# Token-row pairs of 512 columns for the gates, the branch products, the output and the HGRN values of a hybrid decoder layer

## The chip, the core and the metric

The kernel runs on one NeuronCore of a Trainium2 chip. The metric is the device time of one execution in microseconds (us). Lower is better.

## What is computed

One layer reads `x` (256 tokens, 1024 channels), normalises it, multiplies it by one wide input projection, runs three token mixers on slices of the result, gates them, projects each of them, merges the three with sigmoid gates, projects again, normalises and adds `x`. Cut to what matters here:

```
h = rms_norm(x, pre_norm)
z = einsum('btd,dn->btn', h, w_in)                 # 12,848 columns
o_a = nsa_mixer(...)  * silu(a_silu)               # sparse attention, 16 heads
o_b = pool_mixer(...) * silu(b_silu)               # causal pooling
o_c = rms_norm(hgrn2_mixer(q, f_logits, inp, lb))  * silu(c_silu)   # gated recurrence, values inp
y = einsum('btnc,ncd->btnd', stack([o_a, o_b, o_c]), w_branch)
gates = sigmoid(merge_logits)                      # 3 x 1024 columns of z
merged = sum(gates * y)
out = einsum('btd,de->bte', merged, w_out)
x = x + rms_norm(out, post_norm)
```

Everything is float32. A product that has to keep float32 precision is made of three passes on split operands: a value is rounded to a high part (`hH`, `bH`, `WH`) and the rest is a low part (`hL`, `bL`, `WL`), and the product is H times WL plus L times WH plus H times WH.

## The kernel before

The weights are read in 67 slabs, numbered s = 0 to 66 in the order of the list that `plan_slabs` writes. A slab is 1 MB: 1024 rows by 256 columns (`SLAB`), and its product with the 256 tokens is 48 matmuls (2 halves c, 8 row blocks k of 128, 3 passes j). Two slabs at s = 16 and 17, `vwk` and `vw`, are cut the other way: each has half of the rows (4 blocks) of the same 304 columns, so the two together are one product, and each is 24 matmuls.

A product can be laid out in two ways. Feature-major: the weight block is the stationary operand, the 256 tokens stream through, and the result has channels on partitions. Token-major (the kinds in `TOKEN_MAJOR`): 128 tokens of `hH` or `hL` are stationary, the weight columns stream through, and the result has token rows on partitions.

The work of a slab is spread over the engines, each with its own queue, in the order of s:

- SyncE (SP) loads slab s + 3 into `W` when the slab that used the place has been split.
- ScalarE (ACT) makes the high part `WH` (`hi`, L452), and in `read` takes the finished product out of PSUM: a copy, a tanh for the gates (L601) or a square for the last norm (L608). Per slab it runs `mix(s)`, then `read(s)`, then `hi(s + 3)`.
- VectorE (DVE) makes the low part `WL` (`lo`, L662) and the rest of the reads: the SiLU product (L865, L875), the gated branch product (L885) and, in the last branch, its addition to the merged sum `M` (L890).
- GpSimd (POOL) adds the gated products of the first two branches into `M` (`add_merged`, L427), and scales attention probabilities (L414, L417).
- TensorE (PE) runs `mix(s)`, the small matmuls of the mixers, and then `product(s)` (L1030). The recurrence has its turns from s = 9 to 24, the attention heads from s = 32 to 50.

Slab s writes PSUM bank s % 2, so a product waits until slab s - 2 has been read. `M` is held with channels on partitions. Before the output projection, which needs channels on partitions as its stationary operand, `merged_hi` (L546) and `merged_lo` (L756) split `M` into `hH` and `hL`. From s = 51 on no mixer is left: 4 SiLU slabs, then merge and branch slabs in turn up to s = 62, then 4 output slabs. Behind the last product stand, for each of the two token halves, a square (L644), a sum (L964), the product with the norm's gain (L965), a root (L646), a reciprocal (L967), two scaled additions (L970) and the stores.

Of the kernel before, what the change touches and what calls it, by code (L numbers as in the profile page):

```python
# [36 lines left out]
HALF_K = KC // 2  # L37

# [32 lines left out]
LAST = NS - 5  # L71
# [5 lines left out]
ACT_READS = [sum(x[0] in BY_ACT for x in SLABS[:i + 1]) for i in range(NS)]  # L77
DVE_READS = [sum(x[0] in BY_DVE for x in SLABS[:i + 1]) for i in range(NS)]
# [15 lines left out]
def trunk(nc, x, small, consts, w_in, cmp_w, pool_w, w_branch, w_out, post_norm, out):  # L94
# [14 lines left out]
    with ctx:  # L109
# [60 lines left out]
        M = R[:, 3, :].rearrange("p (c t) -> p c t", c=KC)  # L170
# [66 lines left out]
        s_px, s_gg = sem("pool_out"), sem("gates_done")  # L237
        s_fin, s_lbd, s_fin_ss = sem("final"), sem("lb_ready"), sem("out_squares")
# [3 lines left out]
        def slab_source(s):  # L242
# [4 lines left out]
            if kind in TWO_BANKS:  # L247
                part = D // 2 * TWO_BANKS.index(kind)
                return src[part:part + D // 2, col:col + WIDE].rearrange("(k p) n -> p k n", p=P)
            return src[:, col:col + SLAB].rearrange("(k p) n -> p k n", p=P)  # L250

        def slab_view(slot, s):

            if SLABS[s][0] in TWO_BANKS:
                return slot.rearrange("p k n -> p (k n)")[:, 0:HALF_K * WIDE].rearrange("p (k n) -> p k n", n=WIDE)
# [11 lines left out]
        def last_rows(i):  # L267

            return ps[:, (NS - 1) % 2 if i == 0 else 2, 0:SLAB]
# [70 lines left out]
        def _(pool):  # L340
# [80 lines left out]
            def add_merged(b, n):  # L421
                k = 4 * (2 - b) + n
                pool.wait_ge(s_read_v, DVE_READS[WHERE[("branch", n, b)]])
                m = M[:, 2 * n:2 * n + 2, :].rearrange("p c t -> p (c t)")
                if b < 2:
                    pool.wait_ge(s_madd, k - 3)
                    pool.tensor_tensor(m, m, U, ALU.add).then_inc(s_madd, 1)  # L427
                else:
                    pool.tensor_copy(m, U).then_inc(s_madd, 1)
# [10 lines left out]
        def _(act):  # L440
# [13 lines left out]
            def mix(s):  # L454
# [76 lines left out]
                if s >= 1 and SLABS[s - 1][0] == "silu":  # L531
# [3 lines left out]
                    if b < 2:  # L535
                        act.wait_ge(s_prod, WHERE[("branch", 3, b + 1)] + 1)
                    act.activation(bH[:, 2 * n:2 * n + 2, :].rearrange("p c t -> p (c t)"), BR[:, k % 2, :],
                                   ACT.Copy).then_inc(s_bhi, 1)
                if s == LAST:
                    for n in range(3):  # L540
                        merged_hi(n)

            def merged_hi(n):
                act.wait_ge(s_mfin, n + 1)
                act.wait_ge(s_prod, WHERE[("merge", 3, 0)] + 1)
                act.activation(hH[:, 2 * n:2 * n + 2, :].rearrange("p c t -> p (c t)"),  # L546
                               M[:, 2 * n:2 * n + 2, :].rearrange("p c t -> p (c t)"),
                               ACT.Copy, scale=0.5).then_inc(s_mhi, 1)

            def read(s):  # L550
                kind, n = SLABS[s][:2]
                if kind not in BY_ACT:
                    return
                act.wait_ge(s_prod, s + 1)
# [3 lines left out]
                elif kind == "hv":  # L558
                    act.activation(HV[:, :, SLAB * n:SLAB * n + SLAB], b2, ACT.Copy).then_inc(s_read_a, 1)
# [36 lines left out]
                elif kind in ("silu", "merge"):  # L596
                    if s == WHERE[("silu", 0, 2)]:
                        act.wait_ge(s_hn, HG)
                    if s >= WHERE[("silu", 2, 2)]:
                        act.wait_ge(s_read_v, DVE_READS[s - 1] - (0 if SLABS[s - 1][0] == "branch" else 1))  # L600
                    act.activation(TG[:, tslot(s), :], bank(s), ACT.Tanh, scale=0.5).then_inc(s_read_a, 1)  # L601
                else:
                    if n:
                        act.wait_ge(s_read_a, ACT_READS[s - 1])
                    else:
                        act.activation(st_q[:, 0:1], st_eps, ACT.Sqrt)
                    for i in range(TT):
                        last = act.activation(PP[:, i, 0:256], bank(s)[:, 256 * i:256 * i + 256], ACT.Square,  # L608
                                              accum_out=st_o[:, i, n:n + 1])
                    last.then_inc(s_read_a, 1)  # L610
# [22 lines left out]
            for s in range(NS - 1):  # L633
                mix(s)
                read(s)
                if s == LAST:
                    merged_hi(3)
# [4 lines left out]
            for i in range(TT):  # L642
                act.wait_ge(s_last, i + 1)
                act.activation(PP[:, i, 0:256], last_rows(i), ACT.Square, accum_out=st_o[:, i, 3:4]).then_inc(s_osq, 1)  # L644
# [5 lines left out]
        def _(dve):  # L650
# [45 lines left out]
            def mix(s):  # L696
# [53 lines left out]
                if s == LAST:  # L750
                    for n in range(3):
                        merged_lo(n)

            def merged_lo(n):
                dve.wait_ge(s_mhi, n + 1)
                dve.scalar_tensor_tensor(out=hL[:, 2 * n:2 * n + 2, :].rearrange("p c t -> p (c t)"),  # L756
                                         in0=M[:, 2 * n:2 * n + 2, :].rearrange("p c t -> p (c t)"), scalar=0.5,
                                         in1=hH[:, 2 * n:2 * n + 2, :].rearrange("p c t -> p (c t)"),
                                         op0=ALU.mult, op1=ALU.subtract).then_inc(s_mlo, 1)
# [84 lines left out]
            def read(s):  # L844
                kind, n = SLABS[s][:2]
                if kind not in BY_DVE:
                    return
                dve.wait_ge(s_prod, s + 1)
                if kind in ("q", "ks", "kw", "silu", "branch", "out"):
                    dve.wait_ge(s_read_a, ACT_READS[s if kind != "branch" else s - 1])  # L850
                b = bank(s)
                b2 = b.rearrange("p (c t) -> p c t", c=2)
# [7 lines left out]
                elif kind == "silu":  # L860
                    br = SLABS[s][4]
                    k = 4 * (2 - br) + n
                    if br < 2 and n == 0:
                        dve.wait_ge(s_madd, 4 * (2 - br))
# [6 lines left out]
                    if br == 1:  # L871
                        dve.wait_ge(s_px, 4)
                    if k >= 2:
# [3 lines left out]
                elif kind == "branch":  # L877
                    br = SLABS[s][4]
                    k = 4 * (2 - br) + n
                    if k:  # L880
                        dve.wait_ge(s_madd, min(k, 8))
                    if k > 8:
                        dve.wait_ge(s_mfin, k - 8)

                    dve.scalar_tensor_tensor(out=U, in0=TG[:, tslot(s - 1), :], scalar=1.0, in1=b, op0=ALU.add,  # L885
                                             op1=ALU.mult).then_inc(s_read_v, 1)
                    if br == 0:
                        dve.wait_ge(s_read_v, DVE_READS[s])
                        m = M[:, 2 * n:2 * n + 2, :].rearrange("p c t -> p (c t)")
# [419 lines left out]
```

## Time and profile before

| what | value |
|---|---|
| time, median of 3 runs | 480.6 us (480.55 to 480.81) |
| the profiled execution's own time | 480.7 us |
| span of the profiled execution | 478.8 us |
| TensorE busy | 471.5 us, 98% of the span |
| VectorE busy | 347.8 us, 73% |
| ScalarE busy | 278.0 us, 58% |
| GpSimd busy | 170.0 us, 35% |
| data moved | 76.47 MB, 160 GB/s |

The span runs from the first to the last instruction. The time has 1.9 us more than the span in that execution. A busy share says how long at least one instruction was in flight. It does not say how well a matmul used the array.

### The profile page before, as it was taken

To read this page: it belongs to the slowest core of one execution; us is meant where nothing else is said; L and a number is where in the kernel's file an instruction comes from. 1 tells how busy PE (TensorE), PEld (TensorE's weight loads), DVE (VectorE), ACT (ScalarE), POOL (GpSimd) and SP (SyncE) were. 2 spreads that over 40 slices of the span, in tenths; PEclk is the share of its full clock that TensorE was granted. 3 is DMA by queue.
4 is the path that set the end of the run, shared out by engine and by line. 5 is a ranking of instruction groups with operands and counts; after the bars stand their busy time and mean duration, and the time that the engine had idled before them with its cause. 6 is when DMAs were issued, how large, how long until landed. Compare 5 with 4: busy or idle time off the path is not lost.

```text
span 478.8 us, 9549 instructions
## 1 busy us (share of the span) xinstructions
PE 471.5 (98%) x3884; PEld 459.6 (96%) x3884; DVE 347.8 (73%) x611; ACT 278.0 (58%) x418; POOL 170.0 (35%) x157
## 2 busy tenths in 40 slices
PE   9999999999999999999999999999999999999995
PEld 8999999999999999999999999999999999999995
DVE  4999999667987967796996567887674357655654
ACT  6886936599593738563665454665654345333531
POOL 1075290823800019991264615435755020000000
PEclk9999999999999999999999999999999999999999
DMA  9955743415543496355283532252535545577502
GB/s 296 324 165 182 225 134 130 141 54 175 177 144 122 142 266 210 99 174 179 88 252 104 166 97 89 90 175 89 176 96 169 177 152 192 185 244 241 175 1 90
DMA packets 75994, 76.47 MB, mean 160 GB/s; under 512 B 5745, under 2 KB 74609, under 8 KB 75950
## 3 DMA queue, kind: packets, MB, share of 16 engines
q1 hardware_dynamic: 75662, 75.68, 50.5%
q8 instruction: 31, 0.51, 0.5%
q10 hardware_dynamic: 288, 0.18, 0.1%
q14 instruction: 13, 0.11, 0.1%
HBM read 74.81 MB, written 1.05 MB: 158 GB/s over the span
## 4 chain that ended last, share of the span: by engine, by line
PE 88%; DVE 6%; DMA 3%; ACT 2%; issue 1%; SPq 0%; DVEq 0%; ACTq 0%
PE ps L1030 72%; PE ps L1194 3%; DMA W<-w_in 3%; DVE WL L662 2%; PE ps L1052 2%; PE ps L1145 2%; PE ps L1134 1%; PE ps L1161 1%; PE ps L1056 1%; PE ps L1148 1%; PE ps L1071 1%; PE ps L1163 1%; PE ps L1162 1%; PE ps L1099 1%; DVE hL L918 1%
## 5 line engine op out<-in xcount | busy, mean ns | idle before, releaser
L1030 PE MATMUL ps<-hH,WL 128*128 128x256 f32 x688 | 195.7, 288 | 0.6 <-DVE WL L662 0.6
L1030 PE MATMUL ps<-hH,WH 128*128 128x256 f32 x688 | 194.8, 284 | 0.0
L1030 PE MATMUL ps<-hL,WH 128*128 128x256 f32 x688 | 194.8, 284 | 0.0
L662 DVE TENSOR_TENSOR WL<-W,WH 128x2048 fp32r<-128x2048 f32 (+1 forms) x66 | 153.3, 2323 | 17.6 <-PE ps L1030 17.4
L452 ACT ACTIVATE WH<-W 128x2048 fp32r<-128x2048 f32 (+1 forms) x66 | 124.7, 1889 | 37.8 <-PE ps L1030 32.5
L1030 PEld LDWEIGHTS ps<-hH,WL 128*128 128x128 f32 x688 | 130.7, 192 | 2.1 <-DVE WL L662 1.3
L1030 PEld LDWEIGHTS ps<-hL,WH 128*128 128x128 f32 x688 | 131.8, 192 | 0.8 <-issue 0.7
L1030 PEld LDWEIGHTS ps<-hH,WH 128*128 128x128 f32 x688 | 131.8, 192 | 0.0
L414 POOL TENSOR_SCALAR R<-R,st 128x256 f32<-128x256 f32 x32 | 29.2, 923 | 76.8 <-DVE st L841 76.8
L1030 PE MATMUL ps<-bH,WL 128*128 128x256 f32 x192 | 54.9, 286 | 0.0
L1030 PE MATMUL ps<-bH,WH 128*128 128x256 f32 x192 | 54.3, 283 | 0.0
L1030 PE MATMUL ps<-bL,WH 128*128 128x256 f32 x192 | 54.3, 283 | 0.0
L601 ACT ACTIVATE TG<-ps 128x512 f32<-128x512 f32 x24 | 14.4, 600 | 58.9 <-PE ps L1030 58.9
L1030 PE MATMUL ps<-WL,hH 128*128 128x256 f32 (+1 forms) x160 | 46.2, 289 | 0.3 <-DVE WL L662 0.3
L1030 PE MATMUL ps<-WH,hH 128*128 128x256 f32 (+1 forms) x160 | 45.6, 285 | 0.0
L1030 PE MATMUL ps<-WH,hL 128*128 128x256 f32 (+1 forms) x160 | 45.6, 285 | 0.0
L1030 PEld LDWEIGHTS ps<-bH,WL 128*128 128x128 f32 x192 | 36.8, 192 | 0.2 <-issue 0.2
L1030 PEld LDWEIGHTS ps<-bL,WH 128*128 128x128 f32 x192 | 36.8, 192 | 0.1
L1030 PEld LDWEIGHTS ps<-bH,WH 128*128 128x128 f32 x192 | 36.8, 192 | 0.0
L400 POOL TENSOR_TENSOR R<-R 128x510 f32<-128x510 f32 (+3 forms) x10 | 16.9, 1694 | 49.0 <-PE ps L1073 48.3
L417 POOL TENSOR_SCALAR R<-R,st 128x128 f32<-128x128 f32 x32 | 33.9, 1071 | 0.0
L1030 PEld LDWEIGHTS ps<-WL,hH 128*128 128x128 f32 x160 | 30.6, 192 | 1.0 <-DVE WL L662 0.7
(202 smaller groups left out, 786.8 us busy)
## 6 DMA issues: line engine op xcount, KB each, us to landing
W<-w_in SPq DMA_DIRECT2D x48, 1024.0 KB, 5.2
W<-w_branch SPq DMA_DIRECT2D x12, 1024.0 KB, 5.0
W<-w_out SPq DMA_DIRECT2D x4, 1024.0 KB, 5.2
W<-w_in SPq DMA_DIRECT2D x2, 608.0 KB, 3.9
R<-x SPq DMA_DIRECT2D x2, 512.0 KB, 4.3
W<-w_in SPq DMA_DIRECT2D x2, 512.0 KB, 6.5
R<-cmp_w SPq DMA_DIRECT2D x2, 512.0 KB, 8.9
OC<-pool_w SPq DMA_DIRECT2D x4, 256.0 KB, 6.0
```

The costliest lines, as they stand in the source:

```text
L400: link(pool.tensor_tensor(dst[:, :, sh:T], cur[:, :, sh:T], cur[:, :, 0:T - sh], ALU.add))
L414: pool.tensor_scalar(pp[:, 256 * j:256 * j + 256], pp[:, 256 * j:256 * j + 256], w[:, j:j + 1], None, ALU.mult)
L417: last = pool.tensor_scalar(pp[:, 512 + 128 * j:640 + 128 * j], pp[:, 512 + 128 * j:640 + 128 * j], w[:, 2 + j:3 + j], None, ALU.mult)
L452: act.activation(slab_view(WH[:, s % 3], s), slab_view(W[:, s % 3], s), ACT.Copy).then_inc(s_hi, 1)
L601: act.activation(TG[:, tslot(s), :], bank(s), ACT.Tanh, scale=0.5).then_inc(s_read_a, 1)
L662: dve.tensor_tensor(slab_view(WL[:, s % 2], s), slab_view(W[:, s % 3], s), slab_view(WH[:, s % 3], s), ALU.subtract).then_inc(s_lo, 1)
L918: dve.scalar_tensor_tensor(out=hL[:, c, :], in0=ps[:, 2 + c // 2, 256 * (c % 2):256 * (c % 2) + 256], scalar=V[:, V_PRE + c:V_PRE + c + 1] ...
L1030: mm = pe.matmul(o, l, r, start=(at == 0 if mixed else k0 + k == 0 and j == 0), stop=(at == len(order) - 1 if mixed else k0 + k == KC - 1 ...
L1052: pe.matmul(ps[:, b0, 192 * r:192 * r + 192], OWN[e][r][:, hp, t], REACH[e][r][:, hp, 192 * i:192 * i + 192], start=(r == 0), stop=False)
L1056: mm = pe.matmul(ps[:, b0 + 1, P:2 * P], SMALL_K[e][:, hp, t], SMALL_Q[e][:, hp, t], start=True, stop=(i == 0))
L1145: pe.matmul(ps[:, 2, :], queries(h, 1), KS[:, part, g].rearrange("p a t -> p (a t)"), start=(part == 0), stop=(part == 1))
L1194: mm = pe.matmul(ps[64 * hh:64 * hh + 64, 6, at:T], v, p, start=(j == 0), stop=(j == count - 1))
```

## The change

The gates (`mk`, `merge`), the branch products (`bk`, `branch`), the output (`outk`, `out`) and the HGRN values (`hvk`, `hv`) become token-major products of 512 columns, cut in half-depth pairs as `vwk` and `vw` are. A pair shares two PSUM banks, one for each half of the tokens (c = 0, 1). The first of a pair accumulates rows 0 to 511 and is read by nobody; the second adds rows 512 to 1023. Its two halves are read one by one, c = 0 already when the first half of that slab's matmuls is done (`s_half`). The count of slabs (67) and of the bytes is unchanged; 32 slabs are now of 24 matmuls with 512 columns in place of 48 with 256.

The merged sum `M` then has token rows on partitions. TensorE turns it with 16 transposes, 8 ahead of slab 61 and 8 ahead of slab 64 (`TURN_AT`), into PSUM banks 4 to 7, and ScalarE and VectorE make `hH` and `hL` from there. The gated product now goes through `BR` in place of `U`. Which bank a slab half uses is given by `bank_of`.

```diff
-    for n in range(4):
-        out += [("hq", n, "in", C_HQ + n * SLAB), ("hv", n, "in", C_HI + n * SLAB)]
+    for m in range(2):
+        out += [("hq", n, "in", C_HQ + n * SLAB) for n in (2 * m, 2 * m + 1)]
+        out += [(kind, m, "in", C_HI + m * PAIR) for kind in ("hvk", "hv")]
...
-        for n in range(4):
-            out += [("merge", n, "in", C_MERGE + b * D + n * SLAB, b), ("branch", n, b, n * SLAB, b)]
-    out += [("out", n, "out", n * SLAB) for n in range(4)]
+        for m in range(2):
+            out += [(kind, m, "in", C_MERGE + b * D + m * PAIR, b) for kind in ("mk", "merge")]
+            out += [(kind, m, b, m * PAIR, b) for kind in ("bk", "branch")]
+    out += [(kind, m, "out", m * PAIR) for kind in ("outk", "out") for m in range(2)]
...
-TOKEN_MAJOR = ("hv", "vs", "vwk", "vw", "out")
-TWO_BANKS = ("vwk", "vw")
+TWO_BANKS = {"vwk": (0, WIDE), "vw": (1, WIDE), "hvk": (0, PAIR), "hv": (1, PAIR), "mk": (0, PAIR), "merge": (1, PAIR),
+             "bk": (0, PAIR), "branch": (1, PAIR), "outk": (0, PAIR), "out": (1, PAIR)}
+TOKEN_MAJOR = ("vs",) + tuple(TWO_BANKS)
+SPLIT = ("hv", "merge", "branch", "out")
...
+                for m in range(2):
+                    if s == TURN_AT[m]:
+                        act.wait_ge(s_mturn, m + 1)
+                        act.wait_ge(s_prod, WHERE[("merge", 1, 0)] + 1)
+                        for n in (2 * m, 2 * m + 1):
+                            act.activation(hH[:, 2 * n:2 * n + 2, :].rearrange("p c t -> p (c t)"), ps[:, 4 + n, :],
+                                           ACT.Copy, scale=0.5).then_inc(s_mhi, 1)
...
+                if kind in SPLIT:
+                    for c in range(2):
+                        if kind == "merge":
+                            b = SLABS[s][4]
+                            act.wait_ge(s_read_v, DVE_READS[WHERE[("branch", 0, b) if n else ("silu", 3, b)]] - n * (1 - c))
+                        if c:
+                            act.wait_ge(s_prod, s + 1)
+                        else:
+                            act.wait_ge(s_half, HALVES[s])
+                        if kind == "hv":
+                            act.activation(HV[:, c, PAIR * n:PAIR * n + PAIR], rows(s, c), ACT.Copy).then_inc(s_read_a, 1)
+                        elif kind == "merge":
+                            act.activation(TG[:, c, :], rows(s, c), ACT.Tanh, scale=0.5).then_inc(s_read_a, 1)
+                        else:
+                            if c == 0:
+                                act.activation(st_q[:, 0:1], st_eps, ACT.Sqrt)
+                            act.activation(PP[:, c, 0:PAIR], rows(s, c), ACT.Square,
+                                           accum_out=st_o[:, c, 0:1]).then_inc(s_read_a, 1)
...
+            def merge_rows(s, n, br, c):
+                k = 4 * (2 - br) + 2 * n + c
+                dve.wait_ge(s_read_a, ACT_READS[WHERE[("merge", n, br)]] - 1 + c)
+                if k >= 2:
+                    dve.wait_ge(s_madd, min(k - 1, 8))
+                dve.scalar_tensor_tensor(out=BR[:, c, :], in0=TG[:, c, :], scalar=1.0, in1=rows(s, c), op0=ALU.add,
+                                         op1=ALU.mult).then_inc(s_read_v, 1)
+                if br == 0:
+                    dve.wait_ge(s_read_v, DVE_READS[s] - 1 + c)
+                    dve.wait_ge(s_madd, 8)
+                    m = M[:, c, PAIR * n:PAIR * n + PAIR]
+                    dve.tensor_tensor(m, m, BR[:, c, :], ALU.add).then_inc(s_mfin, 1)
...
+                    if kind in TWO_BANKS and c == 1 and k == 0 and j == 0:
+                        bank_read(s, 1)
...
+                for m in range(2):
+                    if s == TURN_AT[m]:
+                        pe.wait_ge(s_mfin, 2 * m + 2)
+                        for j in range(4):
+                            k = 4 * m + j
+                            for i in range(TT):
+                                mm = pe.transpose(ps[:, 4 + k // 2, 256 * (k % 2) + P * i:256 * (k % 2) + P * i + P],
+                                                  M[:, i, P * k:P * k + P], ident)
+                        mm.then_inc(s_mturn, 1)
...
+TURN_AT = (WHERE[("bk", 1, 0)], WHERE[("outk", 1)])
...
+    if kind in ("hvk", "hv", "vwk", "vw"):
+        return c
+    if kind in ("mk", "merge") and SLABS[s][4] == 0 or kind in ("outk", "out") and n == 0:
+        return 2 + c
+    return 1 - c
```

What stands in ScalarE's queue at the first HGRN values, from the read of the second slab with recurrence columns on, before the change (`R` is the buffer that holds the recurrence's values, and L470 is the exponential over 4096 columns in `mix(6)`):

```order
L559 ACTIVATE R<-ps 128x2x256
L452 ACTIVATE WH<-W 128x2048
L466 ACT_TABLE_LOAD
L466 ACTIVATE CVD<-R 128x2x128
L468 ACTIVATE CVD<-R 128x128 x2
L470 ACTIVATE R<-R 128x4096
L557 ACTIVATE R<-ps 128x512
L452 ACTIVATE WH<-W 128x2048
L559 ACTIVATE R<-ps 128x2x256
L452 ACTIVATE WH<-W 128x2048
```

The same place of the changed kernel:

```order
L580 ACTIVATE R<-ps 128x512
L459 ACTIVATE WH<-W 128x2048
L473 ACT_TABLE_LOAD
L473 ACTIVATE CVD<-R 128x2x128
L475 ACTIVATE CVD<-R 128x128 x2
L477 ACTIVATE R<-R 128x4096
L459 ACTIVATE WH<-W 128x2048
L568 ACTIVATE R<-ps 128x512 x2
L459 ACTIVATE WH<-W 128x2048
```

The read of slab 6 is gone, and the two reads of slab 7 (L568), one for each bank, stand behind the high part of slab 9.

On TensorE, between the first and the second output slab (`outk` 0 and `outk` 1) of the changed kernel, one group of transposes stands (L1124, 8 of them). The rows are the end of the one slab and the start of the other:

```order
L1045 MATMUL ps<-WH,hH 128x512
L1124 MATMUL ps<-K,R 128x128 x8
L1045 MATMUL ps<-WL,hH 128x512
L1045 MATMUL ps<-WH,hL 128x512
L1045 MATMUL ps<-WH,hH 128x512
```

Before, the output slabs follow one another with nothing between them, and each of their rows is half as wide:

```order
L1030 MATMUL ps<-WH,hH 128x256
L1030 MATMUL ps<-WL,hH 128x256
L1030 MATMUL ps<-WH,hL 128x256
L1030 MATMUL ps<-WH,hH 128x256
L1030 MATMUL ps<-WL,hH 128x256
```

The transposes are new in TensorE's queue, and everything behind them moves by what they take.

## Rows read from the trace of the kernel before

**Rows 1.** The page: span, parts 1, 2 (clock) and 4.
```profile
span 478.8 us, 9549 instructions
PE 471.5 (98%) x3884; PEld 459.6 (96%) x3884; DVE 347.8 (73%) x611; ACT 278.0 (58%) x418; POOL 170.0 (35%) x157
PEclk9999999999999999999999999999999999999999
PE 88%; DVE 6%; DMA 3%; ACT 2%; issue 1%; SPq 0%; DVEq 0%; ACTq 0%
```

**Rows 2.** TensorE's own waits: who for whom, total us, times, longest.
```profile
PE ps L1219 <- DVE PM L899: 1.2, 1, 1.2
PE ps L1030 <- DVE WL L662: 0.8, 3, 0.3
```

**Rows 3.** The chain that ended last, in order of time: start, us, what.
```profile
226.30 0.47 PE ps L1145 x2
226.77 0.23 PE ps L1148 x2
...
257.12 0.46 PE ps L1145 x2
...
375.49 98.11 PE ps L1030 x816
```

**Rows 4.** TensorE's timeline, three 256-column matmuls in a row.
```profile
56.69 0.28 PE L1030 MATMUL ps<-WH,hL 128*128 128x256 f32 x1
56.81 0.28 PE L1030 MATMUL ps<-WH,hH 128*128 128x256 f32 x1
56.93 0.28 PE L1030 MATMUL ps<-hH,WL 128*128 128x256 f32 x1
```

**Rows 5.** TensorE's timeline, 304 columns: the second and the 24th of slab 17.
```profile
121.34 0.30 PE L1030 MATMUL ps<-WH,hL 128*128 128x304 f32 x1
...
124.41 0.30 PE L1030 MATMUL ps<-WH,hH 128*128 128x304 f32 x1
```

**Rows 6.** TensorE's timeline: 512 columns, then 256, at slab 32.
```profile
226.14 0.63 PE L1145 MATMUL ps<-KS,QS 128*128 128x512 f32 x2
226.61 0.39 PE L1148 MATMUL ps<-KS,QS 128*128 128x256 f32 x2
226.84 0.28 PE L1030 MATMUL ps<-bH,WL 128*128 128x256 f32 x1
```

**Rows 7.** TensorE's timeline: the first and the sixth of six transposes.
```profile
335.26 0.27 PE L1161 MATMUL ps<-K,R 128*128 128x128 f32 x1
...
335.81 0.27 PE L1163 MATMUL ps<-K,R 128*128 128x128 f32 x1
```

**Rows 8.** ScalarE's timeline from slab 6 to slab 7.
```profile
50.77 3.61 ACT L470 ACTIVATE R<-R 128x4096 f32<-128x4096 f32 x1
54.28 0.57 ACT L557 ACTIVATE R<-ps 128x512 f32<-128x512 f32 x1
54.76 1.90 ACT L452 ACTIVATE WH<-W 128x2048 fp32r<-128x2048 f32 x1
57.13 0.60 ACT L559 ACTIVATE R<-ps 128x512 f32<-128x512 f32 x1 [0.47 <-PE ps L1030]
```

**Rows 9.** The timeline behind the last matmul.
```profile
473.62 0.38 ACT L644 ACTIVATE R<-ps 128x256 f32<-128x256 f32 x1 [1.75 <-PE ps L1030]
474.20 0.41 DVE L965 TENSOR_TENSOR R<-ps,R 128x256 f32<-128x256 f32 x1
474.32 0.29 ACT L646 ACTIVATE st<-st 128x1 f32<-128x1 f32 x1 [0.22 <-DVE st L964]
474.72 0.16 DVE L967 RECIPROCAL st<-st 128x1 f32<-128x1 f32 x1
```

**Rows 10.** Groups by form: ScalarE's and VectorE's reads of 512 columns.
```profile
L601 ACT ACTIVATE TG<-ps 128x512 f32<-128x512 f32 x24 | 14.4, 600 | 58.9 <-PE ps L1030 58.9
L895 DVE TENSOR_TENSOR R<-ps,R 128x512 f32<-128x512 f32 x3 | 2.1, 692 | 7.4 <-PE ps L1030 5.6 <-issue 1.8
```

**Rows 11.** The timeline in an attention slab whose product starts at 336.62.
```profile
336.62 0.28 PE L1030 MATMUL ps<-hH,WL 128*128 128x256 f32 x1
338.90 2.28 DVE L662 TENSOR_TENSOR WL<-W,WH 128x2048 fp32r<-128x2048 f32 x1
340.54 0.21 ACT L523 ACTIVATION_READ_ACCUMULATOR R<-ps,st 128x1 f32 x1
```

More of the change, by code:

```diff
@@ L37 @@
 HALF_K = KC // 2
+PAIR = 2 * SLAB
 K_MASK, K_BLOCK, K_ID, K_ONE = 0, 384, 512, 640
@@ L247, in slab_source @@
             if kind in TWO_BANKS:
-                part = D // 2 * TWO_BANKS.index(kind)
-                return src[part:part + D // 2, col:col + WIDE].rearrange("(k p) n -> p k n", p=P)
+                half, wide = TWO_BANKS[kind]
+                return src[D // 2 * half:D // 2 * half + D // 2, col:col + wide].rearrange("(k p) n -> p k n", p=P)
             return src[:, col:col + SLAB].rearrange("(k p) n -> p k n", p=P)
@@ L595, in read @@
                     last.then_inc(s_read_a, 1)
[L596 removed]
+                elif kind == "silu":
                     if s == WHERE[("silu", 0, 2)]:
                         act.wait_ge(s_hn, HG)
[L599 to L600 removed]
+                    if n >= 2:
+                        act.wait_ge(s_read_v, DVE_READS[s - 2])
+                    elif SLABS[s][4] < 2:
+                        act.wait_ge(s_read_v, DVE_READS[WHERE[("branch", 1, SLABS[s][4] + 1)]] - 1 + tslot(s))
                     act.activation(TG[:, tslot(s), :], bank(s), ACT.Tanh, scale=0.5).then_inc(s_read_a, 1)
[L602 to L610, printed above, removed]
             act.dma_start(K[:, K_ID:K_CMASK], consts[:, K_ID:K_CMASK]).then_inc(s_small, 16)
@@ L847, in read @@
                     return
+                if kind in SPLIT:
+                    for c in range(2):
+                        if c:
+                            dve.wait_ge(s_prod, s + 1)
+                        else:
+                            dve.wait_ge(s_half, HALVES[s])
+                        if kind == "branch":
+                            merge_rows(s, n, SLABS[s][4], c)
+                        else:
+                            dve.wait_ge(s_read_a, ACT_READS[s] - 1 + c)
+                            dve.wait_ge(s_post, 16)
+                            dve.tensor_tensor(Y[:, c, PAIR * n:PAIR * n + PAIR], rows(s, c),
+                                              POST[:, PAIR * n:PAIR * n + PAIR], ALU.mult).then_inc(s_read_v, 1)
+                    return
                 dve.wait_ge(s_prod, s + 1)
-                if kind in ("q", "ks", "kw", "silu", "branch", "out"):
-                    dve.wait_ge(s_read_a, ACT_READS[s if kind != "branch" else s - 1])
+                dve.wait_ge(s_read_a, ACT_READS[s])
                 b = bank(s)
-                b2 = b.rearrange("p (c t) -> p c t", c=2)
                 if kind == "q":
@@ L978, in compressed_scores, with bank_read @@
                 return pe.matmul(o, queries(h, i), CKS[:, :, h // HPG, :], start=(h == 0), stop=(h == HEADS - 1))
+            def bank_read(s, c):
+                if s < 2 or SLABS[s][0] in TWO_BANKS and TWO_BANKS[SLABS[s][0]][0]:
+                    return
+                r, rc = BANK_BEFORE[s][c]
+                if r is None:
+                    return
+                part = 1 - rc if SLABS[r][0] in SPLIT else 0
+                if SLABS[r][0] in BY_ACT:
+                    pe.wait_ge(s_read_a, ACT_READS[r] - part)
+                if SLABS[r][0] in BY_DVE:
+                    pe.wait_ge(s_read_v, DVE_READS[r] - part)
             def product(s):
@@ L1031, in product @@
                                    stop=(at == len(order) - 1 if mixed else k0 + k == KC - 1 and j == 2))
-                    if small:
+                    if kind in SPLIT and s < NS - 1 and c == 0 and k == deep - 1 and j == 2:
+                        mm.then_inc(s_half, 1)
+                    while small and (len(order) - 1 - at) * TT * HEADS < len(small) * len(order):
                         i, h = small.pop(0)
@@ L1239, with bank_of, bank_before @@
 LO_AHEAD = tuple(WHERE[key] for key in (("q", 2), ("ks", 0), ("kw", 0)))
+TURN_AT = (WHERE[("bk", 1, 0)], WHERE[("outk", 1)])
+def bank_of(s, c):
+    kind, n = SLABS[s][:2]
+    if kind not in TWO_BANKS:
+        return s % 2
+    if kind in ("hvk", "hv", "vwk", "vw"):
[3 more added lines that the diff above has]
+    return 1 - c
+def bank_before(s, c):
+    for r in range(s - 1, -1, -1):
+        for rc in range(2 if SLABS[r][0] in TWO_BANKS else 1):
+            if bank_of(r, rc) == bank_of(s, c):
+                return r, rc
+    return None, 0
+BANK_BEFORE = [[bank_before(s, c) for c in range(2)] for s in range(NS)]
 def tslot(s):
```

136 lines of the change are left out of this document (46 added, 90 removed).

## The prediction

> **What bounds the kernel now.** I read the page first. TensorE is busy for 98% of the span at the full clock (2.4 GHz) in every slice, and it makes 88% of the chain that ended last [rows 1]. Then I asked what TensorE itself waits for: 2.0 us in all, of which 1.2 us is at the very start [rows 2]. So there is nearly nothing to gain by ending waits, and what counts is how much time TensorE's queue needs by itself. The chain of waits says it most plainly for the last part: 816 matmuls of L1030, 17 slabs of 48, take 98.11 us with nothing between them [rows 3]. That is 0.120 us for each, and the timeline shows the same step between neighbours [rows 4]. The array needs 256 / 2.4 GHz = 107 ns for 256 columns, so each matmul of the main product carries about 13 ns that are not columns.
>
> The change keeps the number of columns and halves the number of matmuls in 32 of the 67 slabs. So its gain is whatever part of those 13 ns goes with the matmul and not with the column.
>
> **The price of a 512-column matmul.** This is the term on which all depends, and the main product has no row for it. Three rows come near.
>
> - At 304 columns the main product steps by (124.41 - 121.34) / 22 = 139.5 ns [rows 5]. From 256 to 304 that is 19.5 ns for 48 columns, 0.406 ns a column. Carried on, 512 columns would take 120 + 256 x 0.406 = 224 ns.
> - At 512 columns the attention scores (L1145, the same split operands) step by (226.61 - 226.14) / 2 = 235 ns [rows 6]. In the chain the 16 pairs of them are 0.47 us 14 times and 0.46 us twice [rows 3], a mean of 234 ns for one.
> - Their 256-column neighbours (L1148) take 0.23 us for two, 115 ns each, with the starts at 226.61 and 226.84 [rows 3, 6].
>
> The last two and the 304-column step lie on one line through zero: about 0.457 ns a column gives 117, 139 and 234 ns. Only the 120 ns of the long streams of 256 columns lie above it, as they would if there the load of the stationary operand sets the step and from 304 columns on the moving columns do. That story explains all four rows, the straight line through 120 and 139.5 explains two. I take **234 ns**. The lower bound is 224 ns; the upper bound is 240 ns, twice the step of 256 columns.
>
> The Trainium skill ("TensorE: Matmul & The Clock Gate", Back-to-back issue gap) gives N / 2.4 + 2.5 ns for a gap, so a pair of 256 would cost only 2.5 ns more than one of 512. By that the change would save 768 x 2.5 = 1.9 us (an estimate from that page of the Trainium skill) and not what the rows give. The same rule of the Trainium skill gives 109 ns for 256 columns, where this trace has 120 ns [rows 4], so the trace disagrees and I go by the rows.
>
> **The sum.**
>
> - *Removed:* 32 slabs x 48 = 1536 matmuls of 120 ns become 768 of 234 ns. One of 512 saves 240 - 234 = 6 ns, so 768 x 6 = **4.6 us** (0.144 us a slab). All of it lies on TensorE's queue, which is the path.
> - *Added:* 16 transposes. The six of an attention head step by (335.81 - 335.26) / 5 = 110 ns [rows 7]. 16 x 0.11 = **1.75 us**, on the path, since TensorE has nothing else to do there.
> - *A wait at slab 8.* ScalarE is busy with the long exponential until 50.77 + 3.61 = 54.38 [rows 8]. After the change it makes the high part of slab 9 next (1.90 us, to 56.3) and then reads the first bank of slab 7 (0.6 us [rows 10]), done at 56.9. Before, slab 8 needed only the read of slab 6, done at 54.85, and its product started at 56.93 [rows 4, 8]. The two narrower-stepped slabs 6 and 7 would let it start 2 x 0.144 = 0.29 us earlier, at 56.64, but it has to wait for that read and starts at about 57.0. Price **0.36 us**. The waiting reads are behind the exponential; what is queued behind them is the high part of slab 10, which is not needed before slab 10.
> - *The tail.* The last square is now over 512 columns: 0.60 for 0.38 us [rows 9, 10], 0.22 us. The product with the gain is 0.69 for 0.41 us [rows 9, 10]; before, it ended level with the root at 474.61, and the reciprocal followed, so its 0.28 us are added too. **0.50 us.** The first token half has 12 x 0.234 = 2.8 us of matmuls over it and stays off the path.
> - *The transposes' neighbours.* The second group needs the last addition into `M`, about 0.07 + 0.69 + 0.69 = 1.5 us behind slab 62, and slab 63 covers it for 5.6 us. Behind the group ScalarE makes one high part (1.9 us) and two copies (1.2 us), VectorE follows with 0.7 us: about 4 us, under slab 64's 5.6 us. Without that cover it would be 4 us on the path. The first group has two slabs more of cover. I price both at nothing.
> - *The reads in halves.* In an attention slab whose product starts at 336.62, the exponentials end at 340.54 + 0.21 = 340.75 [rows 11]. A gate slab's first half would be done at 336.62 + 2.8 = 339.4, so its tanh (0.6 us) would run from 340.8 to 341.4, and the next product begins no earlier than 336.62 + 5.6 = 342.2. So it is covered by 0.8 us. The second bank has another 2.8 us. The low part of the next slab (to 341.18) does not move. Nothing.
> - *Loads.* The same number of slabs of the same size; the part of the chain that is DMA is 3%, at the start [rows 1]. Nothing.
>
> 4.6 - 1.75 - 0.36 - 0.50 = 2.0 us less. The profiled execution took 480.7 us, which becomes 478.7; it stands 0.1 us above the median of the runs, so I predict **478.6 us**. A measurement of this kernel can tell about 0.2% (1 us) from no change, so 2.0 us (0.4%) is seen, if narrowly.
>
> **The rivals.**
>
> *A. The forecast*, with its own range 477.3 to 479.8 us from 232 to 236 ns a matmul (768 x 2 ns = 1.5 us either way, less at the upper end). Chance 0.60.
>
> *B. The 13 ns go with the matmul.* Then 512 columns cost 224 to 226 ns. For it: the 304-column step, which is the only wide one of the main product itself. Against it: both rows of the attention scores. A step of 225 saves 768 x 15 = 11.5 us, less 2.6 us of additions: 471.7 us, and 473 us with some of it lost in waits. Chance 0.17.
>
> *C. More waits like that of slab 8.* TensorE's queue gets shorter while ScalarE's and VectorE's work stays, and every product of a pair waits for a read twice. Around slabs 16 to 18 and 29 TensorE already waits a little for VectorE's low part (three times, 0.8 us [rows 2]), and the gates' first tanh stands behind the exponentials with only 0.8 us of cover. If five or six slabs lose 0.3 us each, 1.7 us are gone: 480.3 us, no change. Against it: most slabs start well behind their low part, and an earlier TensorE lets VectorE start earlier too. Chance 0.13.
>
> *D. Slower: a 512-column matmul costs two of 256.* If the 120 ns are a rate of the moving stream, 512 columns take 240 ns, nothing is saved, and the additions of 1.75 + 0.36 + 0.50 = 2.6 us stand alone; without savings slab 8 loses 0.1 and not 0.36 us, so 480.6 + 2.35 = 483.0 us. It decides from (1.75 + 0.5 + 0.36) / 768 = 3.4 ns a matmul on: above 236.6 ns the kernel is slower. For it: two small readings lie on either side (235 and 234 ns), both within 3 ns of that point, and they come from pairs, not from a long stream. Between 236.6 and 240 ns lies the milder form, in which a small part goes with the matmul: at 237.5 ns the saving is 768 x 2.5 = 1.9 us against 2.5 us of additions, 481.2 us. The rule of the Trainium skill ("TensorE: Matmul & The Clock Gate", Back-to-back issue gap) would give this milder form. Chance 0.10 for both, 0.03 of it for the milder.
>
> **How the numbers follow.** The likeliest case is A, 478.6 us. Most of B lies below 472.5 only if nothing at all is lost, and D lies above 481; a range of 472.5 to 481.0 us leaves out part of B and most of D, about 2 in 10. Faster by over 0.2% (under 479.6 us): nine tenths of A and all of B and the rest a little of C, 0.74. Within 0.2%: the upper edge of A and most of C, 0.15. Slower: D and a part of C, 0.11.
>
> **What would show it.** The step of the 512-column matmuls in a run without mixers, slabs 55 to 60: 234 ns, 5.62 us a slab, where 5.76 stood. The transposes: two blocks of 0.9 us. A gap of about 0.35 us ahead of slab 8, released by ScalarE's read. The time from the last matmul to the first of the last additions: 1.8 for 1.3 us. TensorE's waits in all: about 2.4 us for 2.0. The prediction is wrong if the step is off by more than 2 ns, or if TensorE's waits come to 4 us or more.

## The result and the profile after

The changed kernel takes **475.5 us** (median of 4 runs, 475.17 to 475.63) where the kernel before, run beside it, takes 480.6 us (480.55 to 480.81). The ratio is 0.9892, 95% interval 0.9880 to 0.9904: 5.1 us less. The prediction was 478.6 us, so the direction is right and the time lies in the stated range, but the gain is 2.5 times the forecast of 2.0 us. The profiled execution took 475.2 us.

The page of the changed kernel, the lines that answer to [rows 1]:

```profile
span 473.3 us, 8023 instructions
PE 464.3 (98%) x3132; PEld 419.6 (89%) x3132; DVE 346.8 (73%) x610; ACT 277.8 (59%) x410; POOL 164.1 (35%) x157
PE 83%; DVE 9%; ACT 3%; issue 3%; DMA 1%; SPq 0%; DVEq 0%; ACTq 0%
```

TensorE is still the bound, and its clock is the full one in all 40 slices. Its work is 7.2 us shorter (464.3 for 471.5), the span only 5.5 us. The chain now has 3% of "issue", which was 1%. So there are two things to read: why TensorE's work fell by more than the forecast 4.6 - 1.75 = 2.85 us, and where 1.7 us of what it saved went.

TensorE's timeline where slab 55 ends and slab 56 begins, gate slabs without mixers (start, duration, what):

```profile
405.60 0.39 PE L1045 MATMUL ps<-WH,hH 128*128 128x512 f32 x1
405.82 0.39 PE L1045 MATMUL ps<-WL,hH 128*128 128x512 f32 x1
...
406.28 0.39 PE L1045 MATMUL ps<-WH,hH 128*128 128x512 f32 x1
```

The step is (406.28 - 405.60) / 3 = 227 ns. The prediction took 234. Slabs 56 to 59 start at 405.82, 411.26, 416.70 and 422.14: 5.44 us a slab where 48 x 0.12 = 5.76 us stood, 0.32 us less (forecast: 0.144). That is 512 / 2.4 GHz = 213.3 ns and 13.3 ns more, the same 13 ns that a 256-column matmul carries.

TensorE's waits, the view of [rows 2]:

```profile
PE ps L1045 <- issue: 1.2, 1, 1.2
PE ps L1245 <- DVE PM L914: 1.2, 1, 1.2
PE ps L1045 <- DVE WL L674: 0.5, 2, 0.3
PE ps L1045 <- ACT R L568: 0.3, 1, 0.3
```

3.2 us for 2.0 us. The 0.3 us for ScalarE's read L568 is the forecast one, ahead of slab 8. The 1.2 us in the first row is new and was not forecast. The profile names no engine for it ("issue"). It stands ahead of slab 33 (the first branch half, `bk` 0 of branch 2), between the score matmuls and the product:

```profile
231.18 0.70 PE L1171 MATMUL ps<-KS,QS 128*128 128x512 f32 x2
231.72 0.39 PE L1174 MATMUL ps<-KS,QS 128*128 128x256 f32 x2
233.32 0.47 PE L1045 MATMUL ps<-WL,bH 128*128 128x512 f32 x1 [1.21 <-issue]
```

ScalarE at the same moment (in square brackets the idle time ahead and what ended it):

```profile
232.13 0.60 ACT L537 ACTIVATE CP<-CP 128x480 f32<-128x480 f32 x1 [1.04 <-DVE CP L822]
232.64 1.07 ACT L570 ACTIVATE TG<-ps 128x512 f32<-128x512 f32 x2
```

L537 is the exponential of the compressed scores (the attention scores against the compressed keys). It stands in `mix(32)`, behind the attention's exponentials and ahead of slab 32's reads. ScalarE stands idle for 1.04 us until VectorE has the scores ready, then takes 0.5 us for them, and only then comes the tanh (L570) that frees the banks of slab 32. With 512 columns in two banks, the pair that follows needs the very banks of the pair ahead, so slab 33 waits for the reads of slab 32. Before, L530 (its old line) waited the same 1.04 us, ended by VectorE's L812, and nobody minded: slab 33's product had started at 233.28, since slab s only needed the read of slab s - 2.

```profile
233.28 0.28 PE L1030 MATMUL ps<-hH,WL 128*128 128x256 f32 x1
233.37 0.60 ACT L530 ACTIVATE CP<-CP 128x480 f32<-128x480 f32 x1 [1.04 <-DVE CP L812]
```

The rest in short. Ahead of slab 8, on TensorE and on ScalarE (compare [rows 4, 8]):

```profile
55.72 0.39 PE L1045 MATMUL ps<-WH,hH 128*128 128x512 f32 x1
56.43 0.36 PE L1045 MATMUL ps<-hH,WL 128*128 128x256 f32 x1 [0.33 <-ACT R L568]
...
50.39 3.62 ACT L477 ACTIVATE R<-R 128x4096 f32<-128x4096 f32 x1
53.92 1.90 ACT L459 ACTIVATE WH<-W 128x2048 fp32r<-128x2048 f32 x1
55.72 1.05 ACT L568 ACTIVATE R<-ps 128x512 f32<-128x512 f32 x2
```

The order is the one foreseen: exponential, high part of slab 9, then the reads. Slab 7 starts at 50.51, so it takes 56.43 - 50.51 = 5.92 us, 0.48 more than 5.44. The transposes in the chain that ended last:

```profile
433.19 0.87 PE ps L1124 x8
...
450.42 0.87 PE ps L1124 x8
```

109 ns each, 1.74 us in all, and the view of the waits has none behind them. The tail, beside [rows 9]:

```profile
467.24 0.39 PE L1045 MATMUL ps<-WH,hH 128*128 128x512 f32 x1
467.66 0.60 ACT L656 ACTIVATE R<-ps 128x512 f32<-128x512 f32 x1 [1.39 <-PE ps L1045]
...
469.37 1.41 DVE L983 SCALAR_TENSOR_TENSOR R<-R,st 128x512 f32<-128x512 f32 x2
```

From the start of the last matmul to the last additions it is 469.37 - 467.24 = 2.13 us. Before, the last matmul started at 473.31 and the additions at 474.92, 1.61 us: 0.52 us more.

### The profile page after: what moved, and what is told of

It reads as the page before. It is cut to its first block, busy times and chain, and to the rows that moved or that the text cites. A ratio compares the mean times of both kernels' runs of the same rounds, so it can differ in the third digit from the quotient of the medians.

```text
span 473.3 us, 8023 instructions
## 1 busy us (share of the span) xinstructions
PE 464.3 (98%) x3132; PEld 419.6 (89%) x3132; DVE 346.8 (73%) x610; ACT 277.8 (59%) x410; POOL 164.1 (35%) x157
## 4 chain that ended last, share of the span: by engine, by line
PE 83%; DVE 9%; ACT 3%; issue 3%; DMA 1%; SPq 0%; DVEq 0%; ACTq 0%
PE ps L1045 67%; DVE WL L674 4%; PE ps L1220 3%; PE ps L1069 2%; PE ps L1171 2%; PE ps L1160 1%; DMA W<-w_in 1%; ACT WH L459 1%; PE ps L1187 1%; PE ps L1073 1%; DVE OC L681 1%; DVE R L684 1%; PE ps L1174 1%; PE ps L1088 1%; PE ps L1189 1%
## 5 line engine op out<-in xcount | busy, mean ns | idle before, releaser
L1045 PE MATMUL ps<-hH,WL 128*128 128x256 f32 x496 | 140.5, 289 | 0.9 <-DVE WL L674 0.5
L1045 PE MATMUL ps<-hH,WH 128*128 128x256 f32 x496 | 139.7, 283 | 0.0
L1045 PE MATMUL ps<-hL,WH 128*128 128x256 f32 x496 | 139.7, 283 | 0.0
L1045 PEld LDWEIGHTS ps<-hH,WH 128*128 128x128 f32 x496 | 94.9, 191 | 0.0
L1045 PE MATMUL ps<-WL,hH 128*128 128x512 f32 (+2 forms) x192 | 73.3, 382 | 0.0
L1045 PE MATMUL ps<-WH,hH 128*128 128x512 f32 (+2 forms) x192 | 72.4, 377 | 0.0
L1045 PE MATMUL ps<-WH,hL 128*128 128x512 f32 (+2 forms) x192 | 72.4, 377 | 0.0
L1045 PE MATMUL ps<-WL,bH 128*128 128x512 f32 x96 | 38.2, 398 | 1.2 <-issue 1.2
L1045 PE MATMUL ps<-WH,bH 128*128 128x512 f32 x96 | 37.4, 390 | 0.0
L1045 PE MATMUL ps<-WH,bL 128*128 128x512 f32 x96 | 37.4, 389 | 0.0
```

The lines of the kernel that those rows point to most:

```text
L1045: mm = pe.matmul(o, l, r, start=(at == 0 if mixed else k0 + k == 0 and j == 0), stop=(at == len(order) - 1 if mixed else k0 + k == KC - 1 ...
```

## The experiments

Seven kernels, each the changed kernel with one edit, the last with two. The kernel before was run beside them: 480.73 us (median of 7 runs) for experiments 1, 2, 4 and 5, 480.74 us (9 runs) for 3, 6 and 7. Times are medians; `ruler` and `ruler_bursts` were run once each and are read by their timelines.

### 1. Does the gain go with the number of matmuls? (`halves`)

```diff
-                    mm = pe.matmul(o, l, r, start=..., stop=...)
+                    if kind in TWO_BANKS and TWO_BANKS[kind][1] == PAIR:
+                        pe.matmul(o[:, 0:SLAB], l, r[:, 0:SLAB], start=begin, stop=False)
+                        mm = pe.matmul(o[:, SLAB:PAIR], l, r[:, SLAB:PAIR], start=False, stop=end)
```

> Each matmul of 512 columns is issued as two of 256 with the same stationary block, into the same bank; all else is the changed kernel, same output. If about 13 ns go with every matmul (512 columns step by 226.7 ns in the trace of the changed kernel, 256 columns by 120 ns), 768 more matmuls cost 768 x 13.3 = 10.2 us: 475.5 + 10.2 = 485.7 us. If the gain of the change came from other things (fewer waits, larger pieces of the loads) and the width gave only the 6 ns of the prediction, 475.5 + 4.6 = 480.1 us.

Measured 483.95 us (483.92 to 484.15), 8.4 us over the changed kernel; its span, 482.1 us, is 8.8 us longer. TensorE in slab 50:

```profile
378.36 0.28 PE L1048 MATMUL ps<-WH,bL 128*128 128x256 f32 x1
378.48 0.28 PE L1049 MATMUL ps<-WH,bL 128*128 128x256 f32 x1
378.60 0.28 PE L1048 MATMUL ps<-WH,bH 128*128 128x256 f32 x1
```

The step is 0.12 us again, although neighbours now share their stationary operand. Layout, order and loads are those of the changed kernel, so the width alone is worth 8.4 us, 10.9 ns for each of the 768 matmuls that were split. This kernel is 3.2 us slower than the kernel before (483.95 for 480.73): that is what the rest of the change costs, the transposes (1.7), the wait ahead of slab 33 (1.0 here) and the tail (0.5). A clean slab loses 0.32 us (5.76 for 5.44). The difference to 10.2 us is in the slabs where TensorE also waits or has small matmuls: slab 7 got 0.16 us shorter (its wait is gone), slab 32 did not change (its wait takes the difference in), slab 31 lost 0.14 us, and most slabs beside the attention heads 0.26 to 0.30 us.

One thing stays open. Every matmul has a load of its stationary operand of its own (PEld), also where the neighbour uses the same one: the page of `halves` has 768 more of both, PE and PEld x3900 for x3132. No kernel here leaves a load out, so the 13 ns may belong to the matmul or to its load.

### 2. The step by width and by operand (`ruler`)

Nine streams of 12 matmuls with no other purpose stand ahead of slab 51. The line numbers in the timeline below are theirs.

```diff
+                for _ in range(12):
+                    pe.matmul(ps[:, 2, 0:512], queries(15, 1), keys, start=True, stop=True)
+                for _ in range(12):
+                    pe.matmul(ps[:, 2, 0:512], hH[:, 0, 0:P], keys, start=True, stop=True)
...
```

> Nine streams of 12 matmuls each stand ahead of slab 51, where no mixer is left; their results are not used. They change one thing at a time: the stationary block (attention queries or hH), the moving operand (attention keys or the high part of a weight slab) and the width. If the fixed part goes with the matmul, the steps are n / 2.4 + 13: 226.7 ns for 512, 173 for 384, 139.7 for 304, 120 for 256, and 107 to 120 for 192, where the load of the stationary block takes over; and keys as moving operand give 227 too, so that the 234 ns of the score pairs come from their short bursts. If the score pairs are slow because of their operands, the streams with keys or with queries step by 234 ns and those with hH and weights by 227. The rival of the prediction (0.457 ns a column) would give 234, 175 and 139 ns with any operand. Time: 108 matmuls, some 21 us more, 497 us.

Measured 494.64 us. TensorE's timeline:

```profile
377.93 2.88 PE L1171 MATMUL ps<-KS,QS 128*128 128x512 f32 x12
380.65 2.88 PE L1173 MATMUL ps<-KS,hH 128*128 128x512 f32 x12
383.37 2.88 PE L1175 MATMUL ps<-WH,QS 128*128 128x512 f32 x12
386.09 2.88 PE L1177 MATMUL ps<-WH,hH 128*128 128x512 f32 x12
388.81 2.27 PE L1179 MATMUL ps<-WH,hH 128*128 128x384 f32 x12
390.92 1.81 PE L1181 MATMUL ps<-WH,hH 128*128 128x304 f32 x12
392.57 1.59 PE L1183 MATMUL ps<-WH,hH 128*128 128x256 f32 x12
394.00 1.48 PE L1185 MATMUL ps<-WH,hH 128*128 128x192 f32 x12
395.32 1.61 PE L1187 MATMUL ps<-KS,QS 128*128 128x256 f32 x12
```

The distance of the starts, divided by 12, is the price of one. 512 columns cost 226.7 ns with any of the four pairs of operands; 384 cost 175.8, 304 cost 137.5, 256 cost 119.2 and 120.8, 192 cost 110.0. Score operands are no slower than weights. What is left over the columns themselves (n / 2.4 GHz) is 13.3, 15.8, 10.8, 12.5 and 14.1 ns: 11 to 16 ns from 256 columns on. The spread is that of one run of 12, as single steps scatter after a change of width (0.17 to 0.19 us at 384). The longer rows agree on 13: 120 ns at 256 columns over 816 matmuls [rows 3] leaves 13.3, and 139.5 ns at 304 over 22 steps [rows 5] leaves 12.8. At 192 it is 30 ns, and the step is that of the 128-column transposes [rows 7], so about 110 ns looks like a floor. All 12 matmuls of a stream here use the same stationary block (each with its own load), in the main product every one has another; 226.7 and 120 ns are the same in both. The prediction's story had the floor at 120 ns and the moving columns alone from there on; this falls.

### 3. Where did 234 ns come from? (`ruler_bursts`)

```diff
+                for r in range(6):
+                    for part in range(2):
+                        pe.matmul(ps[:, 2, :], queries(15, 1), both[part], start=(part == 0), stop=(part == 1))
...
+                    for part in range(2):
+                        pe.matmul(diagonal[:, 2:4], queries(15, 0), near[part], start=(part == 0), stop=(part == 1))
...
+                    for k in range(4):
+                        pe.matmul(ps[:, 2, 0:P], ones, ident, start=True, stop=True)
```

> The changed kernel with 96 extra matmuls ahead of slab 51, whose results nobody uses, to find where the 234 ns of the score pairs comes from: 6 pairs of 512 columns with the score operands (two parts of the keys in turn, start and stop), then 6 pairs of 256 columns, then 6 times the burst as the attention heads have it (a pair of 512, a pair of 256), then 6 times four matmuls of 128 columns with six of 512 behind them. Theory (a change of width costs, not the operand): the pure streams step by 227 and by about 120 ns; in the exact burst the 512-column ones take 234 ns and the 256-column ones 115 ns, as in the heads, since the step that the timeline shows for a matmul also holds the load of the one behind it. Rival (the start of a new accumulation or the two parts cost it): the pure stream of score pairs steps by 234 ns already. Sum of the extra work about 19 us, so about 494 us in all by the first, about 0.2 us more by the second.

Measured 497.56 us. TensorE's timeline: the pure streams of pairs, then two of the six bursts, then the last block:

```profile
377.65 2.88 PE L1171 MATMUL ps<-KS,QS 128*128 128x512 f32 x12
380.37 1.60 PE L1174 MATMUL ps<-KS,QS 128*128 128x256 f32 x12
381.81 0.63 PE L1177 MATMUL ps<-KS,QS 128*128 128x512 f32 x2
382.28 0.39 PE L1179 MATMUL ps<-KS,QS 128*128 128x256 f32 x2
382.50 0.63 PE L1177 MATMUL ps<-KS,QS 128*128 128x512 f32 x2
...
385.99 1.06 PE L1182 MATMUL ps<-K 128*128 128x128 f32 x8
386.80 1.63 PE L1184 MATMUL ps<-KS,QS 128*128 128x512 f32 x6
388.27 1.05 PE L1182 MATMUL ps<-K 128*128 128x128 f32 x8
```

The same pairs in a pure stream cost (380.37 - 377.65) / 12 = 226.7 ns and (381.81 - 380.37) / 12 = 120 ns. In the burst the timeline shows 0.47 and 0.22 us, near the 0.47 and 0.23 of [rows 6]. But the six bursts together take (385.99 - 381.81) / 6 = 0.697 us each, and the pure prices give 2 x 226.7 + 2 x 120 = 693 ns. So nothing costs more in a burst. The split at the change of width is moved by some 14 ns: the wide pair looks like 2 x 235 ns, the narrow pair like 2 x 110 to 115. The first theory holds for the prices and says too much with "a change of width costs": it costs 4 ns of 697 at most. Why the starts are shown so is open. The time in all came out 3.6 us above the expected sum. Most of that is the last block: four plain float32 matmuls of 128 columns (operands that were not rounded to a high part) stand as 8 rows and cost (2.28 - 6 x 0.2267) / 4 = 230 ns each and not 110, 24 x 0.12 = 2.9 us more. The other 0.7 us is open.

### 4. The unforeseen wait (`exp_behind`)

ScalarE's exponential of the compressed scores stands behind slab 32's two reads instead of ahead.

```diff
-                if s == SC + 1:
-                    act.wait_ge(s_csm, 1)
...
-                    act.activation(sm, sm, ACT.Exp).then_inc(s_cexp, 1)
...
+                if s == SC + 1:
+                    act.wait_ge(s_csm, 1)
...
+                    act.activation(sm, sm, ACT.Exp).then_inc(s_cexp, 1)
```

> The exponential of the compressed attention scores is moved on ScalarE from ahead of the two tanh reads of slab 32 to behind them; same output. In the trace of the changed kernel slab 33 starts 1.2 us late, released at 233.3 when the first tanh is done, and the tanh stands behind that exponential, which waits for VectorE until 232.1. If that is the cause, the wait goes and 1.2 us come back: 474.3 us. If the second bank or the low part of slab 33 or 34 is next in line, less than 0.5 us comes back.

Measured 474.12 us (473.87 to 474.37), 1.4 us under the changed kernel; the ratio to before is 0.9863, interval 0.9848 to 0.9878. ScalarE and TensorE at the place:

```profile
231.16 1.10 ACT L566 ACTIVATE TG<-ps 128x512 f32<-128x512 f32 x2
232.32 0.61 ACT L649 ACTIVATE CP<-CP 128x480 f32<-128x480 f32 x1
...
231.89 0.40 PE L1174 MATMUL ps<-KS,QS 128*128 128x256 f32 x2
232.13 0.40 PE L1045 MATMUL ps<-WL,bH 128*128 128x512 f32 x1
```

The step from slab 32 to 33 is 6.23 us (7.60 in the changed kernel, 6.44 before), and "issue" is gone from TensorE's waits. So the wait that the profile gave to no engine was for the reads behind that exponential, and its price was 1.4 us, the 1.2 us of the gap and some 0.2 us behind it.

### 5. The transposes twice (`turn_twice`)

```diff
-                        for j in range(4):
+                        for j in list(range(4)) * 2:
```

> Each group of 8 transposes is done twice into the same places; same output. If the transposes lie on the path at their own length (0.80 us for a group of 8), the time rises by 1.6 us to 477.1 us. If TensorE would have waited there anyhow for the copies of the merged sum, it rises by less than 0.8 us.

Measured 477.40 us (477.34 to 477.53), 1.9 us more for 16 more, 117 ns each by the medians. In the timeline the doubled group is 16 x 0.109:

```profile
433.44 1.91 PE L1124 MATMUL ps<-K,R 128*128 128x128 f32 x16
435.10 0.48 PE L1045 MATMUL ps<-WL,bH 128*128 128x512 f32 x1
435.41 0.39 PE L1045 MATMUL ps<-WH,bL 128*128 128x512 f32 x1
```

From 433.44 to the second matmul it is 1.97 us; less 0.227 for the first, 1.74 us for 16. The slab in which a group stands gets longer by 7.11 - 6.23 = 0.88 us for 8 more, so by the timeline it is 1.75 us for both groups; the last 0.1 us of the medians lies elsewhere. The term of the sum holds, and with a group twice as long still nobody waits for the split of `M`.

### 6. The HGRN values left single (`hv_single`)

```diff
-    for m in range(2):
-        out += [("hq", n, "in", C_HQ + n * SLAB) for n in (2 * m, 2 * m + 1)]
-        out += [(kind, m, "in", C_HI + m * PAIR) for kind in ("hvk", "hv")]
+    for n in range(4):
+        out += [("hq", n, "in", C_HQ + n * SLAB), ("hv", n, "in", C_HI + n * SLAB)]
```

> This is the changed kernel with one part undone: the HGRN values are four token-major slabs of 256 columns at full depth in the old order (query, value, query, value), as in the kernel before. Everything else stays paired. Theory (the gain of a pair is about 13 ns for each matmul that goes away, 0.32 us a slab): four value slabs lose 4 x 0.32 = 1.28 us, and the wait of 0.50 us ahead of slab 8 is gone, so it takes 0.8 us more than the changed kernel, about 476.3 us, and the slab that follows slab 7 starts without a wait for ScalarE. Rival (the wait at slab 8 costs as much as the four wide slabs gain): no difference, 475.5 us, or less.

Measured 476.21 us (476.08 to 476.31), 0.7 us over the changed kernel. The ratio, 0.9906 (0.9892 to 0.9919), has an interval that overlaps the changed kernel's, but all its runs lie above all of that one's. Slab 8 starts at 56.92 without a wait for ScalarE. So the values' pairs gain about 1.2 us and lose 0.5 at slab 8, as expected.

### 7. Both waits moved out of the way (`two_moves`)

On top of `exp_behind`, ScalarE makes the high part of slab 9 between the two reads of slab 7 and not ahead of both.

```diff
+                            if s == 7 and c == 0:
+                                hi(9)
...
-                if s + 3 < NS:
+                if s + 3 < NS and s != 6:
```

> The changed kernel with two moves in ScalarE's queue: the exponential of the compressed scores stands behind slab 32's two tanh reads (as in the run exp_behind), and in slab 7 the first half's read stands ahead of the high part of slab 9 and the second half's behind it. Theory: the wait ahead of slab 8 (0.50 us) ended with a read that stood behind that high part of 1.9 us; with the move the read is done at about 55.0 and slab 8 starts when slab 7's matmuls end, so the time is 0.4 to 0.5 us under exp_behind, about 473.7 us. Rival 1: the second half's read, which is still behind the high part, is waited for in the middle of slab 8 or by VectorE, and nothing is gained: 474.1 us. Rival 2: the high part of slab 9 is now 0.6 us later and slab 9 waits for it or for its low part: 474.1 to 474.7 us.

Measured **473.46 us** (473.37 to 473.57), 0.66 us under `exp_behind`; ratio to before 0.9849, interval 0.9835 to 0.9862. The interval overlaps that of `exp_behind`, but all runs lie below all of that one's (473.87 to 474.37). ScalarE and TensorE around slab 8:

```profile
54.17 0.58 ACT L564 ACTIVATE R<-ps 128x512 f32<-128x512 f32 x1
54.65 1.91 ACT L459 ACTIVATE WH<-W 128x2048 fp32r<-128x2048 f32 x1
56.45 0.58 ACT L564 ACTIVATE R<-ps 128x512 f32<-128x512 f32 x1
...
55.96 0.39 PE L1047 MATMUL ps<-WH,hH 128*128 128x512 f32 x1
56.18 0.28 PE L1047 MATMUL ps<-hH,WL 128*128 128x256 f32 x1
```

The first read ends at 54.75, and slab 8 starts 0.22 us after the last matmul of slab 7, with no wait. The second read, at 56.45, is needed by nobody before its end. The step of slab 7 is 5.44 us and not 5.93, and slab 8's is 0.06 us shorter: the timelines show 0.55 us, the rest of the 0.66 is not placed. Of the kernels run this is the fastest, 7.3 us under the kernel before.

## Why the prediction was off, step by step

- **"The price of a 512-column matmul. ... I take 234 ns": this step failed.** The reason for it, that from 304 columns on the moving columns alone set the step at 0.457 ns a column, was wrong: some 13 ns go with each matmul (and its load) at every width from 256 on. The price is 226.7 ns. The saving of a clean slab is 0.32 us and not 0.144, in 32 slabs 10.2 us and not 4.6. The rival B had this mechanism and came within a nanosecond or two (224 to 226 ns). The prediction gave the two readings of the attention scores more weight than the one wide row of the main product. Experiment 2 shows that the operands don't matter, experiment 3 that the 234 ns were a share of a burst and no price. The trace of before could have told it: in [rows 6] the four matmuls take 226.84 - 226.14 = 0.70 us, and two of 256 columns cost 0.24 by [rows 4], which leaves 230 ns. With starts shown to 0.01 us that is sure to some 5 ns only, so it was a hint that 234 is too high and no proof. The prediction read 115 ns for a 256-column matmul whose price it knew to be 120, and took that as support for its line through zero.
- **"The reads in halves. ... Nothing": the second failure, 1.4 us.** The cover of 0.8 us was worked out in one ordinary attention slab. Slab 32 has one instruction more ahead of its reads, and this one waits for VectorE. The prediction looked for slow reads in ScalarE's queue behind the long exponential of slab 6 and did not walk the queue at the other places where something foreign stands ahead of a read of a pair. Its rival C named the gates' first tanh and its thin cover, but as five or six waits of 0.3 us; there was one, of 1.2 us.
- *"Added: 16 transposes", 1.75 us:* measured 1.74 us, 1.9 us when doubled. Right.
- *"A wait at slab 8", 0.36 us:* right in place and cause. It cost 0.48 us, as the faster slabs 6 and 7 would have let slab 8 start earlier still. The start was given as about 57.0 and is 56.43. Some 0.37 us of that is that the slabs ahead came earlier, before any changed slab; the other 0.2 us is that the forecast added durations, where ScalarE starts an instruction about 0.1 us before the end of the one ahead (53.92 for 50.39 + 3.62 = 54.01).
- *"The tail", 0.50 us:* measured 0.52. Right.
- *"The transposes' neighbours" and "Loads", nothing:* TensorE has no wait there. Right.
- *Two slips that moved nothing.* The waits for the low part in [rows 2] are at slabs 4, 5 and 29, and not "around slabs 16 to 18 and 29"; two of the three lie ahead of the first changed slab. And 1.5 us under 478.6 is 477.1, not 477.3, for the lower end of the forecast's own range.
- *What neither the forecast nor B had:* in slab 31, with 32 small score matmuls, the wide step gives only 9.90 - 9.83 = 0.07 us, and beside the attention heads 0.28 us a slab.

The sum with measured terms: 10.2, less 0.25 (slab 31) and about 15 x 0.04 = 0.6 (attention slabs), is 9.4 us; less 1.7 (transposes), 0.5 (slab 8), 1.4 (slab 33) and 0.5 (tail) leaves 5.3 us. The spans differ by 5.5 us, of which 0.35 us lie ahead of slab 4, where nothing was changed (the profiled executions of the experiments start that slab at 33.06 to 33.48, before stands at 33.25, and only this one at 32.90); the medians differ by 5.1 us. B's price with the forecast's other terms would have said 480.6 - 10.2 + 2.6 = 473.0 us, too little by the 1.4 us of slab 33 and the 0.9 us of slab 31 and the attention slabs. So it is in part luck that 475.5 us lies so near the middle of the stated range: the gain that was priced too low and the wait that was priced at nothing point opposite ways. By the prediction's own sign, a step off by more than 2 ns, it was wrong: the step is off by 7 ns. Its other sign, waits of 4 us or more, did not come (3.2 us).

The Trainium skill ("TensorE: Matmul & The Clock Gate", Back-to-back issue gap) gives N / 2.4 + 2.5 ns, and gives it for a matmul by itself. For a stream in which each matmul has its weight load it says that both set the spacing, and names about 131 ns for 512 columns. By the formula a 512-column matmul would save 2.5 ns against two of 256; here it saves 2 x 120 - 226.7 = 13.3 ns. The trace agrees with neither figure: with these split float32 operands and a load for each matmul it shows 226.7 ns for 512 columns, and a rule of the same form with about 13 ns (11 to 16) in place of 2.5, from 256 columns on.

## What to carry to other kernels

Take the price of an instruction from a long run of its own kind, and test a reading from a short burst against the sum of the whole burst. Where the chain is TensorE's queue, fewer and wider matmuls pay by a fixed amount for each that goes, here 13 ns where nothing else stands in the way and 11 ns on the whole. When two products come to share a bank pair in direct succession, walk the reading engine's queue at every place where something else stands ahead of a read, above all something that waits itself: that wait was harmless with one slab of distance and cost 1.4 us without.

## What the runs showed of the hardware

- TensorE's step in a stream where each matmul has its own load of the stationary operand: 110.0 ns at 192 columns, 119 to 121 at 256, 137.5 at 304, 175.8 at 384, 226.7 at 512, at the full clock. At 512 columns neither the source of the operands nor the accumulation flags changed it, and a new stationary operand each time (the main product) or always the same one (`ruler`) gave the same step.
- Matmuls that share their stationary operand with their neighbour (experiment 1) still step by 120 ns, each with its own load.
- A plain float32 matmul of 128 columns takes two rows and 230 ns; a transpose of the same size takes one row and 109 ns.
- At a change of width the starts in the timeline are shifted by about 14 ns, so that the sum is right and the parts are not.
